# Triangular inverses in a two-block transformer kernel: levels 2 to 16 on 32x32 tiles of TensorE in place of 64x64

## What is computed

```python
A = jnp.where(strict, bc[..., :, None] * kk * decay, 0.0) + jnp.eye(C)
u = lax.linalg.triangular_solve(A, bc[..., None] * vc, left_side=True, lower=True, unit_diagonal=True)
w = lax.linalg.triangular_solve(A, bc[..., None] * jnp.exp(G)[..., None] * kc, ...)
```

## Time and profile before

| | |
|---|---|
| median of three runs | 2714.75 us |
| the profiled execution | 2715.86 us |
| its span in the profile | 2714.0 us |
| TensorE busy | 2500.2 us, 92% |
| VectorE busy | 1812.8 us, 67% |
| ScalarE busy | 1419.7 us, 52% |
| HBM, mean over the span | 210 GB/s |

### The profile page before, as it was taken

The page is one execution under the profiler, slowest core; times in us unless marked ns, Lnnn a source line. Parts: engine busy times, 40 slices in busy tenths (PEclk is TensorE's granted clock), DMA queues, the critical chain, the costliest instruction groups (busy, mean ns, idle before and its releaser), DMA issues. The chain is left out here.

```text
span 2714.0 us, 39934 instructions
## 1 busy us (share of the span) xinstructions
PE 2500.2 (92%) x15196; PEld 2105.9 (78%) x15196; DVE 1812.8 (67%) x2467; ACT 1419.7 (52%) x1894; POOL 315.4 (12%) x207
## 2 busy tenths in 40 slices
PE   8788989999898999979998987799999999999998
PEld 6458659989885799756997976688888888888886
DVE  3665445558575555374556745788888888988886
ACT  4242234445552444153445522477777777777775
POOL 3110200004542000000003421000000000000000
PEclk9889799999899999969998998899999999999999
DMA  6610125544332355413554400799999999999995
GB/s 247 199 62 2 52 78 197 185 140 147 120 112 75 107 185 173 159 62 114 184 170 171 153 2 1 293 374 371 381 368 370 381 365 380 365 376 377 372 365 219
DMA packets 180011, 573.86 MB, mean 211 GB/s; under 512 B 11966, under 2 KB 81726, under 8 KB 136764
## 3 DMA queue, kind: packets, MB, share of 16 engines
q1 hardware_dynamic: 175932, 558.27, 55.5%
q0 software_dynamic: 2992, 11.01, 1.6%
q10 hardware_dynamic: 976, 3.03, 0.3%
HBM read 564.16 MB, written 6.29 MB: 210 GB/s over the span
## 5 line engine op out<-in xcount | busy, mean ns | idle before, releaser
L3420 DVE TENSOR_TENSOR moe_weights_low<-ring,moe_weights_high 128x1024 fp32r<-128x1024 f32 x672 | 782.2, 1217 | 103.5 <-ACT moe_weights_high L3657 100.7
L3657 ACT CAST moe_weights_high<-ring 128x1024 fp32r<-128x1024 f32 x672 | 686.6, 1053 | 109.1 <-PE banks L258 105.5
L256 PE MATMUL banks<-moe_weights_high,moe_rows_high 128*128 128x512 f32 x896 | 354.6, 396 | 3.1 <-DVE moe_rows_low L3425 2.5
L258 PE MATMUL banks<-moe_weights_low,moe_rows_high 128*128 128x512 f32 x896 | 350.2, 391 | 0.0
L257 PE MATMUL banks<-moe_weights_high,moe_rows_low 128*128 128x512 f32 x896 | 349.5, 390 | 0.0
L256 PE MATMUL banks<-ffn_x_high,ffn_weights_high 128*128 128x256 f32 x1056 | 299.0, 283 | 0.7 <-DVE ffn_x_low L3043 0.7
L257 PE MATMUL banks<-ffn_x_high,ring_low 128*128 128x256 f32 x1056 | 297.5, 282 | 0.0
L258 PE MATMUL banks<-ffn_x_low,ffn_weights_high 128*128 128x256 f32 x1056 | 297.4, 282 | 0.0
L3219 DVE TENSOR_TENSOR ring_low<-ring,ffn_weights_high 128x2048 fp32r<-128x2048 f32 x60 | 134.8, 2288 | 126.9 <-ACT ffn_weights_high L3193 126.9
L256 PEld LDWEIGHTS banks<-ffn_x_high,ffn_weights_high 128*128 128x128 f32 x1056 | 199.2, 189 | 4.2 <-DVE ffn_x_low L3043 1.3
L257 PEld LDWEIGHTS banks<-ffn_x_high,ring_low 128*128 128x128 f32 x1056 | 199.4, 189 | 2.7
(11 more groups left out here) (617 smaller groups left out, 4766.3 us busy)
## 6 DMA issues: line engine op xcount, KB each, us to landing
ring<-in_moe_gate_pieces SPq DMA_DIRECT2D x112, 1024.0 KB, 7.0
ring<-in_moe_up_pieces SPq DMA_DIRECT2D x112, 1024.0 KB, 7.2
ring<-in_moe_down_pieces SPq DMA_DIRECT2D x112, 1024.0 KB, 7.1
ring<-in_ffn_w SPq DMA_DIRECT2D x66, 1024.0 KB, 7.8
ring<-in_od_w_in SPq DMA_DIRECT2D x10, 2048.0 KB, 8.3
ring<-in_o_w_in SPq DMA_DIRECT2D x8, 2048.0 KB, 8.5
ring<-in_e_ffn_w_gate SPq DMA_DIRECT2D x11, 1024.0 KB, 5.4
ring<-in_e_ffn_w_up SPq DMA_DIRECT2D x11, 1024.0 KB, 8.0
```

The lines of the kernel that those rows point to most:

```text
L256: pe.matmul(out_, lh, rh, start=start, stop=False)
L258: return pe.matmul(out_, lh, rl, start=False, stop=stop)
L3420: dve.tensor_tensor(lo[:, b], piece, hi[:, b].bitcast(F32), ALU.subtract).then_inc(sems["lo_done"], 1)
L3657: act.copy(hi[:, b * 1024:(b + 1) * 1024], piece).then_inc(sems["hi_done"], 1)
```

## The change

Levels 2, 4, 8 and 16 work on 32-row blocks, four for each head, each 32x32 on a quarter of its own on the array's diagonal. The tiles are half as wide (128 columns for four heads) and there are 16 matmuls in place of 8 for each step. At level 16 the last product also gets the blocks themselves, as a second matmul into the same place of PSUM, and is laid out in 64-row blocks: two copies by VectorE and two by ScalarE, of 32 rows each, bring it into the other half of tile X, which two memsets a call have set to zero. Level 32 and the joining work on 64-row blocks in the second halves of the tiles, as before. The constants lose 192 columns (masks and identity 32 wide).

```diff
@@ -53,10 +53,12 @@
     parts["upto_mid"] = (p <= f) * 1.0 - (p < P // 2)
     parts["halves"] = np.stack([np.arange(P) < P // 2, np.arange(P) >= P // 2], 1)
     parts["after_neg"] = np.where(p <= f, 0.0, NEG)
-    row, col = p % 64, f[:, 0:64]
-    parts["ident64"] = (row == col)
-    parts["pair64"] = (row // 2 == col // 2) & (row % 2 == 0) & (col % 2 == 1)
+    row, col = p % 32, f[:, 0:32]
+    parts["ident32"] = (row == col)
+    parts["pair32"] = (row // 2 == col // 2) & (row % 2 == 0) & (col % 2 == 1)
     for s in LEVELS:
+        if s == 32:
+            row, col = p % 64, f[:, 0:64]
         parts[f"level{s}"] = (row // (2 * s) == col // (2 * s)) & (row % (2 * s) >= s) & (col % (2 * s) < s)
     parts["quad"] = np.concatenate([p < f, p <= f, p < f, p <= f], 1)
     parts["causal"] = np.where(k <= q, 0.0, NEG).reshape(P, TT * T)
@@ -1124,27 +1126,31 @@
         def invert(groups, during={}, clear=False):
 
             r4 = lambda ap: ap.rearrange("p (g n) -> p g n", g=4)
-            wide = lambda ap: ap.unsqueeze(1).to_broadcast([P, 4, 64])
+            wide = lambda ap, n: ap.unsqueeze(1).to_broadcast([P, 4, n])
             sides = (slice(0, 64), slice(64, 128))
-            col = lambda j: slice(j * 64, (j + 1) * 64)
+            tiles = tuple(slice(q * 32, (q + 1) * 32) for q in range(4))
+            col = lambda j, n=64: slice(j * n, (j + 1) * n)
+            blocks_of = {32: slice(0, 128), 64: slice(256, 512)}
+
             for g in groups:
-                g["blocks"], g["blocks_t"], g["low"] = (g[name][:, 0:256] for name in ("X", "NL", "Y"))
                 @block.vector
                 def _(dve):
                     for due in unseen(dve, g["ready"]):
                         dve.wait_ge(*due)
-                    for b in sides:
-                        dve.tensor_tensor(r4(g["blocks_t"])[b], g["NT"][b, :, b],
-                                          const("pair64")[b].unsqueeze(1).to_broadcast([64, 4, 64]), ALU.mult).then_inc(*V.tick())
+                    turned = r4(g["NL"][:, blocks_of[32]])
+                    for b in tiles:
+                        dve.tensor_tensor(turned[b], g["NT"][b, :, b], const("pair32")[b].unsqueeze(1).to_broadcast([32, 4, 32]),
+                                          ALU.mult).then_inc(*V.tick())
                     dve.wait_ge(*V.at())
-                    dve.tensor_tensor(r4(g["blocks_t"]), r4(g["blocks_t"]), wide(const("ident64")), ALU.add).then_inc(*V.tick())
+                    dve.tensor_tensor(turned, turned, wide(const("ident32"), 32), ALU.add).then_inc(*V.tick())
                 g["turned"] = V.at()
-            if clear:
-                for g in groups:
-                    @block.vector
-                    def _(dve):
+            for g in groups:
+                @block.vector
+                def _(dve):
+                    dve.memset(g["X"][:, blocks_of[64]], 0.0).then_inc(*V.tick())
+                    if clear:
                         dve.memset(r4(g["XT"])[64:128, :, 0:64], 0.0).then_inc(*V.tick())
-                    g["cleared"] = V.at()
+                g["cleared"] = V.at()
             for g in groups:
                 bank = take_bank()
 
@@ -1153,8 +1159,8 @@
                     for due in unseen(pe, bank.free, g["turned"]):
                         pe.wait_ge(*due)
                     for j in range(4):
-                        for b in sides:
-                            last = pe.matmul(bank.ap[b, col(j)], g["blocks_t"][b, col(j)], ident[b, b], start=True, stop=True)
+                        for b in tiles:
+                            last = pe.matmul(bank.ap[b, col(j, 32)], g["NL"][b, col(j, 32)], ident[b, b], start=True, stop=True)
                     last.then_inc(*M.tick())
                 turned = M.at()
 
@@ -1163,10 +1169,14 @@
                     for due in unseen(act, g["ready"]):
                         act.wait_ge(*due)
                     act.wait_ge(*turned)
-                    act.copy(g["blocks"], bank.ap[:, 0:256]).then_inc(*S.tick())
+                    act.copy(g["X"][:, blocks_of[32]], bank.ap[:, 0:128]).then_inc(*S.tick())
                 bank.free = g["have"] = S.at()
             for n, s in enumerate(LEVELS):
+                size = 64 if s == 32 else 32
+                cuts = sides if s == 32 else tiles
+                widen = s == 16
                 for g in groups:
+                    X, XT, Y = (g[name][:, blocks_of[size]] for name in ("X", "NL", "Y"))
                     if n:
                         bank = take_bank()
 
@@ -1175,15 +1185,15 @@
                             for due in unseen(pe, bank.free, g["have"]):
                                 pe.wait_ge(*due)
                             for j in range(4):
-                                for b in sides:
-                                    last = pe.matmul(bank.ap[b, col(j)], g["blocks"][b, col(j)], ident[b, b], start=True, stop=True)
+                                for b in cuts:
+                                    last = pe.matmul(bank.ap[b, col(j, size)], X[b, col(j, size)], ident[b, b], start=True, stop=True)
                             last.then_inc(*M.tick())
...
                             act.wait_ge(*turned)
-                            act.copy(g["blocks_t"], bank.ap[:, 0:256]).then_inc(*S.tick())
+                            act.copy(XT, bank.ap[:, 0:4 * size]).then_inc(*S.tick())
                         bank.free = g["turned"] = S.at()
                     bank = take_bank()
 
@@ -1192,38 +1202,64 @@
                         for due in unseen(pe, bank.free, g["have"]):
                             pe.wait_ge(*due)
                         for j in range(4):
-                            for b in sides:
-                                last = pe.matmul(bank.ap[b, col(j)], g["NT"][b, j, b], g["blocks"][b, col(j)], start=True, stop=True)
+                            for b in cuts:
+                                last = pe.matmul(bank.ap[b, col(j, size)], g["NT"][b, j, b], X[b, col(j, size)], start=True, stop=True)
                         last.then_inc(*M.tick())
...
                         dve.wait_ge(*have)
-                        dve.tensor_tensor(r4(g["low"]), r4(bank.ap[:, 0:256]), wide(const(f"level{s}")), ALU.mult).then_inc(*V.tick())
+                        dve.tensor_tensor(r4(Y), r4(bank.ap[:, 0:4 * size]), wide(const(f"level{s}"), size), ALU.mult).then_inc(*V.tick())
                     bank.free = g["low_have"] = V.at()
                 for g in groups:
+                    X, XT, Y = (g[name][:, blocks_of[size]] for name in ("X", "NL", "Y"))
                     bank = take_bank()
+                    place = lambda j, q: col(j, 32) if not widen else slice(j * 64 + q % 2 * 32, j * 64 + q % 2 * 32 + 32)
 
...
                         for j in range(4):
-                            for b in sides:
-                                last = pe.matmul(bank.ap[b, col(j)], g["blocks_t"][b, col(j)], g["low"][b, col(j)], start=True, stop=True)
+                            for q, b in enumerate(cuts):
+                                out_ = bank.ap[b, place(j, q) if size == 32 else col(j)]
+                                last = pe.matmul(out_, XT[b, col(j, size)], Y[b, col(j, size)], start=True, stop=not widen)
+                            if widen:
+                                for q, b in enumerate(cuts):
+                                    last = pe.matmul(bank.ap[b, place(j, q)], XT[b, col(j, 32)], ident[b, b], start=False, stop=True)
                         last.then_inc(*M.tick())
                     have = M.at()
-
-                    @block.vector
-                    def _(dve):
-                        for due in unseen(dve, g["have"]):
-                            dve.wait_ge(*due)
-                        dve.wait_ge(*have)
-                        dve.tensor_tensor(g["blocks"], g["blocks"], bank.ap[:, 0:256], ALU.add).then_inc(*V.tick())
-                    bank.free = g["have"] = V.at()
+                    if widen:
+                        whole = g["X"][:, blocks_of[64]]
+                        pieces = [(b, slice(q % 2 * 32, q % 2 * 32 + 32)) for q, b in enumerate(tiles)]
+
+                        @block.vector
+                        def _(dve):
+                            dve.wait_ge(*have)
+                            for b, c in pieces[0:2]:
+                                dve.tensor_copy(r4(whole)[b, :, c], r4(bank.ap[:, 0:256])[b, :, c]).then_inc(*V.tick())
+
+                        @block.scalar
+                        def _(act):
+                            for due in unseen(act, g["cleared"]):
+                                act.wait_ge(*due)
+                            act.wait_ge(*have)
+                            for b, c in pieces[2:4]:
+                                act.copy(r4(whole)[b, :, c], r4(bank.ap[:, 0:256])[b, :, c]).then_inc(*S.tick())
+                        bank.free = g["have"] = [V.at(), S.at()]
+                    else:
```

(9 more changed lines are left out.)

## The result

The changed kernel takes 2758.09 us (median of 5 runs, 2748.56 to 2759.16) against 2715.97 for the kernel before on the same chip (5 runs, 2714.60 to 2717.42): a ratio of 1.0149, 95% interval 1.0137 to 1.0160, so 42 us slower. The forecast was 2701.8, with a range to 2719: wrong in sign and outside. The first rival, "TensorE can't start instructions fast enough", had given 2752.

A forecast was written before the change was run, and what follows sets the result against it. TensorE was taken to bound the inverses, with VectorE and ScalarE waiting for it. Gains of 2.05, 3.8, 3.9 and 3.3 us in the four calls, together 13.0, took 2714.75 to 2701.8 us; range 2699 to 2719.

The forecast's parts named there:

- The first rival: TensorE's queue in the calls: twice the instructions can't start fast enough, 37 us slower, 2752 us; chance 0.20.
- a block on quarters: TensorE's 16 matmuls of 32 columns: 32 records in 8 rounds of four, 0.24 us for 0.465 at full clock.
- I take 0.24: Choice of block time between 0.24 and 0.93 us, from rows where a third tile starts with two others, 19 ns a record.
- the other bound, 0.93: Upper bound of a small-tile block: 32 records at 29 ns, if they can't come faster for long than in the old levels.
- Level 32 and the end stay: 0: Last level of the inverse and what follows, on the old tiles: no change in time.
- today's spacing is set by columns: Argument against an instruction limit: the old levels' 14.5 ns an instruction comes from matmul and load widths.
- The Trainium skill: Cited guide: matmuls never start less than about 25 ns apart; across tiles, a block of 0.80 us, kernel 24 us slower.
- A warm level 1.87: Levels 4 and 8 at full clock: the first group's own chain binds, 1.87 us for 3.14, a gain of 1.27.
- level 16 2.45: Level 16, with extra matmuls and 32-row copies in place of one add: 2.45 us, a gain of 0.70.
- The start: From a call's first mask to level 4: 5.7 us, 0.7 less in call 1 and 1.2 less in the others.
- The clock: TensorE's clock in the calls: call 1's rise comes 3.4 us later, the other three calls' rises stay.
- The third rival: Clock does not rise on 32x32 tiles: levels stay at 2.9 us, level 32 gives back 0.6; -1.8, 2713 us; chance 0.08.

The follow-up runs named there:

- after_warm: Changed kernel with ten 128x128 matmuls of 256 columns, result unused, ahead of each call's first turn; 2754.26 us, ratio 1.0138 to the kernel before.
- after_wide: Changed kernel, all four heads, with streams of 64 columns instead of 32 on the small tiles, the second 32 unused; 2758.96 us, ratio 1.0146.
- twice_instr: Kernel before, on its 64x64 tiles, each matmul of levels 2 to 32 cut into two of 32 columns; 2857.08 us, ratio 1.0516.
- half_wide: Changed kernel with only half of the heads multiplied on 32x32 tiles, the others taking copies, and streams of 64 columns; 2708.64 us, ratio 0.9972.
- dve_turn_warm: Kernel before with all turns up to level 32 on VectorE and ten wide matmuls ahead of each call; 2716.01 us, ratio 0.9985.
- pad_small: Kernel before with two extra 32x32 matmuls, result unread, for each head in each step of levels 2 to 32; 2950.64 us, ratio 1.0860.

## Why the prediction was wrong

- **The step that failed: a block on quarters, 0.24 us, in every level.** The row it needed was there for the rounds and the price was right: 0.24 at the upper clock in after_warm, 0.43 at half for 0.46 priced. The step that failed is the one after it, "I take 0.24: the rows with three tiles are the nearer ones". It set the rate of a sustained level by a burst over three rounds. Against the other bound, 0.93 from "records can't come faster for long than in today's levels", the measured levels of call 2, 4.9, 4.5 and 6.7 us, stand at 0.75 to 0.85 a block. What the runs showed in its place is the supply: 256 instructions in about 3.5 us.
- **A second term that failed: "Level 32 and the end stay: 0".** Level 32 has the old tiles and the old number of instructions, and it took 6.58, 6.20, 5.15 and 5.56 us in the four calls for 3.14 before. In call 3 no pause lies in it, and the clock alone is left. That level of call 3, after and then before:

```profile
1631.42:1636.57 5.15, 5.15 (x100) 5.15 (x96) 1.83 (x5) 1.26 (x4) 0.00 (x0) 0.50 0.01 3
```

```profile
1604.08:1607.22 3.14, 2.98 (x70) 2.64 (x65) 1.69 (x4) 1.47 (x4) 0.00 (x0) 1.00 0.00 0
```

- **The first rival** had place and sign, and its size in part by luck. Its level 5.3 measured 4.4 to 6.0, its level 16 of 7.5 measured 6.7 to 7.5. Levels 4 to 16 lost 27.8 us in all, where its own terms add up to about 35 (the prediction says 37); what brought the total near its 2752 is level 32, which it had not. It was given 0.20 on an argument that did not bear on it: "today's spacing is set by columns" is true and says nothing of how close the supply lies behind. The view that the earlier trace rows come from had the answer: fetches in the old levels already come 3.5 to 5 us apart, and the new level of 384 instructions in 1.87 us wanted a piece every 1.25 us, with a landing time of 1.0 us for each. An old level takes 192 instructions in 3.14 us, 16.4 ns each; the supply's 13.6 was close behind it.
- **The Trainium skill** ("TensorE: Matmul & The Clock Gate", section "Wait — 56ns, not 53.3ns?") has a floor of about 25 ns between matmuls. Across tiles it does not hold: 32 records start in 0.24 us, 7.5 ns each. What bound was not the start of a matmul but the arrival of its instruction.
- **A warm level 1.87, level 16 2.45**: never seen with all heads; with half of them level 8 is 2.63, with a wait for instructions in it.
- **The start**: 5.93 us in call 1 (208.60 to 214.53) for 5.7 forecast and 6.39 before; 5.99 in call 2 (260.25 to 266.24) for 5.7 and 6.89; 5.71 in call 4. Right to 0.3 us. These are the instructions that lay ready. In call 3 only 350 lay ready, the first pause fell into the start, and it took 7.05.
- **The clock**: I let one rise come 3.4 us later. It stayed at half for 27.3, 23.9, 30.7 and 27.3 us of the calls. The third rival was right in this. Its time, 2713, assumed levels that TensorE's work sets; with the supply behind them, levels 4 to 16 are no faster at the upper clock.
- **Account.** The calls are longer by 36.7 us, and the pauses are 30.4. By stages, in the four calls together: the start 2.4 us less, level 4 7.4 more, level 8 4.9, level 16 15.5, level 32 10.9, the joining 0.4. In levels 4 to 16 the loss is the supply's: the work between the pauses, slow or fast, fills time that would otherwise be pause. In level 32 the half clock has a share, 2.0 us in call 3; in the other calls a pause of 0.5 to 1.0 us comes on top. How the 10.9 us divide between the two stays open, since no run has level 32 at the upper clock throughout behind levels that wait for instructions.

## What to carry to other kernels

Price a change that cuts matmuls into smaller ones in instructions too: an fp32 matmul here is two matmuls and two weight loads, and TensorE got 256 of these in about 3.5 us. If the new inner loop asks for more than one in 13.6 ns over longer than some 400 instructions (350 to 430 here), expect the supply to set its time, whatever the tiles do. Two rows show it before anything is built: how far apart the instruction fetches of the densest stretch lie, and the records between them. Look at the stage behind the change as well: here level 32, itself unchanged, lost 10.9 us, in part to a clock that had not come back. Where small blocks have to be transposed, VectorE's 32x32 transposition takes instructions and a copy away.

## What the runs showed of the hardware that I had not expected

- The supply does not follow TensorE's clock: where TensorE waits for it, a piece every 3.3 to 3.8 us in the changed kernel, mostly at 0.50, and one every 3.3 to 4.0 us at 1.00 in calls 1 and 2 of after_wide. Why TensorE starts only 1.2 to 1.5 us after a piece has landed, and whether more pieces could be under way, stays open; no run here varied it.
- The granted clock stayed at 0.50 through 40 us in which TensorE had no gap, on streams of 32 columns (twice_instr), and came back to 1.00 in levels 4 and 8 on small tiles with streams of 64 (half_wide, after_wide), in spite of the pauses. In dve_turn_warm it fell to 0.50 for 20.5 us in a stretch of 128-wide matmuls without a gap. What the chip goes by was not looked for.
- A change from 64x64 to 32x32 tiles took 0.24 us and one back 0.17 at half clock (pad_small), up to five rounds of the small tiles. A kernel that changes shape head by head, as that one does, pays it each time.
- On a 64x64 tile a stream of 32 columns costs nearly what one of 64 costs, 107 ns against 115 for a pair at half clock.
